# One 1024-column subtraction in place of two of 512 for the low part of a weight unit

## The reference, cut to what matters

```python
proj = h @ w_in                                     # 39 units of 128 columns in layer 0, 61 in layer 1
xbc  = silu(causal_dwconv(xbc, conv_w, conv_b))     # four taps along the tokens
...                                                 # SSD heads and window attention, or gated DeltaNet and block attention
y    = concatenate([y_a, y_b]) @ w_out              # 2048 x 1024
x    = x + g_m * rms_norm(y, norm_w)
u    = causal_dwconv(h @ w_up, conv_w, conv_b)      # three taps; w_up is 1024 x 5632
y    = (gelu(gate) * val) @ w_down                  # 2816 x 1024
```

## Time and profile before

| | |
|---|---|
| median of 3 runs | 1235.38 us (1235.38 to 1236.77) |
| the profiled execution, its own time | 1234.31 us |
| its span in the trace | 1232.5 us |
| PE busy | 1125.3 us, 91% |
| DVE busy | 883.5 us, 72% |
| ACT busy | 628.2 us, 51% |
| mean granted TensorE clock | 0.953 of 2.4 GHz |

### The profile page before, as it was taken

One profiled execution on the slowest core, in us unless ns is written; L12 is line 12 of the kernel. 1 busy time (PEld: TensorE's weight loads), 2 busy tenths in 40 slices (PEclk: granted clock), 3 DMA queues, 4 the chain that ended last, 5 costly groups with the idle time before them and its releaser, 6 DMA issues.

```text
span 1232.5 us, 28100 instructions
## 1 busy us (share of the span) xinstructions
PE 1125.3 (91%) x10161; PEld 1088.7 (88%) x10161; DVE 883.5 (72%) x1909; ACT 628.2 (51%) x1317; POOL 21.0 (2%) x12
## 2 busy tenths in 40 slices
PE   5899999989899999989999997589986989999996
PEld 5899988979899999989999985579876989999996
DVE  3587646669778889976888674876644886888854
ACT  1376455344366665445666536166524445666542
POOL 0000000000000000000000001200100000000000
PEclk9899899999889999987999998789999998999998
DMA  9457534627636566932766521013202662666661
GB/s 358 151 172 238 177 122 141 197 84 292 254 104 186 178 181 221 342 118 78 228 223 187 188 70 35 2 40 88 83 1 92 208 249 75 184 185 179 180 200 56
DMA packets 54830, 195.58 MB, mean 159 GB/s; under 512 B 6067, under 2 KB 8115, under 8 KB 54492
## 3 DMA queue, kind: packets, MB, share of 16 engines
q1 hardware_dynamic: 54748, 194.45, 48.2%
HBM read 193.36 MB, written 1.07 MB: 158 GB/s over the span
## 4 chain that ended last, share of the span: by engine, by line
PE 68%; DVE 6%; ACT 2%; issue 1%; DVEq 0%; ACTq 0%
PE proj L507 43%; PE acc L507 25%; DVE off_bd L1677 1%; DVE state L1751 1%; PE acc L688 0%; DVE sys_t L1685 0%; DVE yr L1492 0%; DVE o_tok L1778 0%; DVE yr L1469 0%; DVE k_tok L1667 0%; DVE conv L1698 0%; DVE w_lo L1345 0%; ACT w_hi L1003 0%; DVE dec L1660 0%; DVE ada_sum L1359 0%
## 5 line engine op out<-in xcount | busy, mean ns | idle before, releaser
L1003 ACT ACTIVATE w_hi<-raw 128x512 fp32r<-128x512 f32 x528 | 328.7, 625 | 178.6 <-PE acc L507 127.9
L1345 DVE TENSOR_TENSOR w_lo<-raw,w_hi 128x512 fp32r<-128x512 f32 x528 | 358.8, 684 | 79.0 <-ACT w_hi L1003 77.8
L507 PE MATMUL proj<-h_hi,w_hi 128*128 128x256 f32 x1352 | 389.8, 288 | 4.0 <-DVE h_lo L1465 3.7
L507 PE MATMUL proj<-h_lo,w_hi 128*128 128x256 f32 x1352 | 386.1, 286 | 0.0
L507 PE MATMUL proj<-h_hi,w_lo 128*128 128x256 f32 x1352 | 385.9, 285 | 0.0
L507 PEld LDWEIGHTS proj<-h_hi,w_hi 128*128 128x128 f32 x1352 | 262.9, 194 | 6.7 <-issue 4.0
L507 PEld LDWEIGHTS proj<-h_lo,w_hi 128*128 128x128 f32 x1352 | 263.5, 195 | 0.0
L507 PEld LDWEIGHTS proj<-h_hi,w_lo 128*128 128x128 f32 x1352 | 263.1, 195 | 0.0
L507 PE MATMUL acc<-a_hi,w_hi 128*128 128x256 f32 (+1 forms) x608 | 172.5, 284 | 3.6 <-DVE a_lo L1632 2.0
L507 PE MATMUL acc<-a_lo,w_hi 128*128 128x256 f32 (+1 forms) x608 | 170.4, 280 | 0.0
L507 PE MATMUL acc<-a_hi,w_lo 128*128 128x256 f32 (+1 forms) x608 | 170.3, 280 | 0.0
(11 more groups left out here) (259 smaller groups left out, 1564.3 us busy)
## 6 DMA issues: line engine op xcount, KB each, us to landing
raw<-in_w_stream SPq DMA_DIRECT2D x264, 512.0 KB, 3.6
ada_long<-in_ada_stream SPq DMA_DIRECT2D x52, 512.0 KB, 6.9
ada_first<-in_ada_stream SPq DMA_DIRECT2D x20, 512.0 KB, 4.4
ada_ssd<-in_ada_stream SPq DMA_DIRECT2D x12, 512.0 KB, 4.5
ada_out<-in_ada_stream SPq DMA_DIRECT2D x12, 512.0 KB, 4.8
hankel<-bias_scratch SPq DMA_DIRECT2D x2, 1024.0 KB, 6.1
x<-in_x_tiles SPq DMA_DIRECT2D x1, 1024.0 KB, 10.5
out_tiles<-x SPq DMA_DIRECT2D x1, 1024.0 KB, 3.9
```

Of the source, the lines that this page charges most:

```text
L507: return pe.matmul(out, a, b, start=start, stop=stop, skip_group_check=True)
L1003: act.activation(hi, src, ACT.Copy).then_inc(w_rounded, 1)
L1345: dve.tensor_tensor(lo, src, hi.bitcast(F32), ALU.subtract).then_inc(w_split, 1)
```

## The change

`split_half` does nothing any more for half 0. When it is called for half 1 it waits until both halves of the unit are rounded, forms the low part of the whole unit in one instruction of 1024 columns, and adds 2 to `w_split`. The two slots that the unit's halves take in `w_hi` and `w_lo` lie side by side, and so do the halves in `raw`, so one instruction reaches them.

```diff
             def split_half(n, a, i=0):
-                if n >= UNITS:
+
+                if n >= UNITS or a == 0:
                     return
-                hi, lo, src = w_half(n, a)
-                dve.wait_ge(w_rounded, 8 * i + 2 * n + a + 1)
-                dve.tensor_tensor(lo, src, hi.bitcast(F32), ALU.subtract).then_inc(w_split, 1)
+                s = 2 * n % 4
+                dve.wait_ge(w_rounded, 8 * i + 2 * n + 2)
+                dve.tensor_tensor(w_lo[:, s:s + 2].rearrange("p s a b -> p (s a b)"), raw[:, n % 4].rearrange("p a b -> p (a b)"),
+                                  w_hi[:, s:s + 2].rearrange("p s a b -> p (s a b)").bitcast(F32), ALU.subtract).then_inc(w_split, 2)
```

## The result

| | before | after |
|---|---|---|
| median | 1235.41 us (1235.38 to 1236.77) | 1283.68 us (1279.78 to 1289.47) |
| the profiled execution, its own time | 1234.31 us | 1282.69 us |
| its span | 1232.5 us | 1280.5 us |
| mean granted clock | 0.953 | 0.960 |

The change makes the kernel slower by a ratio of 1.0383 (95% interval 1.0356 to 1.0411). The forecast was 1284 us, with a range of 1260 to 1298.

A forecast was written before the change was run, and what follows sets the result against it. PE bounds the kernel (busy 91%, 68% of the chain); later low parts stall it in tap stages. Terms sum to 51 us on 1234.3, 1285.3; adding 1.1 to the median and taking 2 off gave 1284 us, range 1260 to 1298.

The forecast's parts named there:

- LS: Start of PE's last matmul of unit n, from which the low part's ready and due times for unit n+2 are counted.
- The bare tap wait: Conv and up stages: second tap's uncovered wait for the first, pitch 0.64 us against 0.40; ends move sum -7.7 to +7.0.
- The restart from the low part's end: A released PE starts 0.13 us after the low part's end, read at one unrolled place; in loops up to 0.12 more.
- out0: Start of out0, where PE already waits for DVE: half 0 lasts 1.22 in place of 0.70, costing 0.5 us.
- The tap stages in sum: Conv and up stages: 27.2, 7.0 and 12.2 us looped, 2 unrolled, less 2 for first units.
- The start of down1: DVE arrives late from the last up step with four terms a unit: estimated 0.9 us, likewise at down0.
- The SSD steps, the norms and what lies around them: Three norms cost 0.3 us; SSD split delays DVE at most 0.54 us, but PE takes `mmat` 0.59 later.
- The steady steps of out and down: They cost nothing: two steps stay about 6.1 us and the low part is ready 0.6 us ahead of due.
- DVE's saved time counts: Rival, in out and down: DVE holds PE back, saving at most 17 us, time 1231 us; chance 0.05.
- the cover holds: Rival, tap stages: the low part still comes in time, no change, 1234 to 1237 us; chance 0.04.
- Half the stall: Rival, tap stages: tap wait not bare and restart free, 0.18 us a unit in up, 1264 us; chance 0.11.
- The clock: Rival, tap stages: PE's pauses drop the granted clock to 1.2 GHz for parts, 1325 us; chance 0.04.

The follow-up runs named there:

- wide between the taps: Kernel after with the one 1024-column split moved back between first and second tap in conv and up stages: 1250.55 us, ratio 1.0115.
- two halves late: Kernel after with its split made as two 512-column instructions, each with its own signal, both behind the second tap: 1249.43 us, ratio 1.0101.
- one signal: DVE's instructions and order as in the kernel before, but half 0 is signalled only together with half 1: 1271.2 us, ratio 1.0267.
- later in every second: Kernel after with the split moved behind `prod` in the second unit of each pair of the up stages: 1304.78 us, ratio 1.0558.
- after, 8 more matmuls: Kernel after with eight repeated matmuls added to each unit of the conv and up stages: 1375.44 us.
- the pair with more matmuls: Eight repeated matmuls added per conv and up unit, once on the kernel before and once on the kernel after: 1367.29 and 1375.44 us.
- the fourth experiment: 1024-column split only outside conv and up, which keep two halves as in the kernel before: 1238.3 us beside 1238.26 for before, ratio 1.0008.

## Why the prediction was right

The mechanism, its place and its size were right. That the median came within 0.3 us of the forecast is luck: the tap stages lost 44.7 us for 46.4, the rest at least 5.0 for 2.6, and 1.7 of these 5.0 did not show in the span (3.3), where the granted clock was 0.960 and not 0.953. What the rest lost is in part of a kind that the sum had put at nothing.

**The round.** By it two units take the time from LS to the ready low part, plus the time from PE's restart to its next LS. With the two numbers that the trace of after corrected (PE starts 0.05 behind the low part's end, and takes 2.85 from first to last start), every variant follows in up0:

| | low part ready | round | per unit | measured per unit |
|---|---|---|---|---|
| before | LS + 2.35 | 5.20, under 5.76 | 2.88 | 2.878 |
| wide between the taps | LS + 2.95 | 5.80 | 2.90 | 2.930 |
| two halves late | LS + 2.97 | 5.82 | 2.91 | 2.937 |
| one signal | LS + 3.34 | 6.19 | 3.10 | 3.114 |
| after | LS + 3.51 | 6.36 | 3.18 | 3.196 |
| later in every second | LS + 3.98 | 6.83 | 3.42 | 3.420 |
| after, 8 more matmuls | LS + 3.51 | 7.32 (3.51 + 2.85 + 0.96), under 7.68 | 3.84 | 3.838 |

The measured column is the mean over ACT's taps from the fifth to the last. The two variants at LS + 2.95 and 2.97 lose 0.05 to 0.06 us a unit where the due time alone, LS + 3.00, would give nothing: a low part must be there somewhat before the matmul that needs it. The weight load that goes ahead of the matmul is what waits in their traces, by some 0.1 us once in two units. I have no run that tells the size of this lead apart from the restart.

**Point by point.**

- The bare tap wait, taken at 0.64 between 0.52 and 0.75: a pair of taps lasts 1.11, so its pitch is 1.11 - 0.48 = 0.63 in up. In the conv stages it is more, 79.81 - 79.14 = 0.67 (below). The split took 1218 ns for a forecast of 1.22 us.
- The restart from the low part's end, taken from out0 as 0.13, was 0.05 in the loops. This is the term of the sum that was mis-sized most: 0.08 a round, 0.04 a unit, 5 us over 128 units. The second matmul came 0.22 behind the first, not 0.20.
- up: 0.34 a unit forecast, 3.196 - 2.878 = 0.318 measured. conv0: 0.44 and 3.301 - 2.858 = 0.443; the round there gives 3.30 a unit by the corrected terms, and 0.02 of the 0.443 come from before, which took 2.858 and not 2.88. conv1: 0.38 and 3.236 - 2.880 = 0.356.
- The tap stages in sum: 46.4 for the looped units, 2 for the unrolled, less 2 for the first units, is 46.4 against 44.7.
- out0: 0.5 forecast. PE waited 2.26 us where it had waited 1.67, 0.59 more (PE's timeline of the kernel after stands below). The start of down1: 0.9 forecast and some 0.1 for its norm; 78.86 - 77.58 = 1.28 measured. down0 has the same two waits of 0.45 and 0.15 us, yet its stretch came out 0.55 us shorter than before, at a mean clock of 0.93 against 0.90. Its cost can be read at its start, where the clock was 1.00 in both. From up0's last tap to the first matmul behind the second wait it was 480.47 - 472.33 = 8.14 us before and 501.78 - 492.37 = 9.41 after, 1.27 more. In the pair with more matmuls, at 0.93 in both, the whole stretch is 99.68 against 97.82 us.
- The SSD steps, the norms and what lies around them: 0.3 us were forecast for three norms and nothing for the rest. The kernel after has the same delays as the fourth experiment, 0.61 at `ada_sum`, 0.61 at `mmat`, 0.51 at the norm behind conv1 and 0.47 in the attention: 2.2 us. The forecast had read `mmat` as ready 0.59 us ahead of PE in one SSD step. In the step at 202 us it had no such lead, and the split's longer time went to PE whole. One step was not enough to set this term to nothing.
- The steady steps of out and down: two steps of DVE take 6.1 us, from the split at 302.57 to the second next at 308.66 below, as forecast, and PE does not wait there. PE's own pace is 2.82 us a unit there, 5.63 for two, so that DVE falls behind by 0.46 in two steps, before as after; the stage ends before that costs a wait for the split.
- Waits in one unit of two, which was one of the two forms named. Their total, forecast as some 45 us, is 40.4 by the weight loads' row and 27.2 by PE's.

PE's timeline of the kernel after at the start of out0:

```profile
288.43 0.36 PE L507 MATMUL acc<-a_hi,w_hi 128*128 128x256 f32 x1 [2.26 <-DVE w_lo L1346]
```

DVE's timeline of the kernel after, in conv0 and in out0:

```profile
79.14 0.48 DVE L1400 SCALAR_TENSOR_TENSOR conv<-proj,prm,conv 128x255 f32 x1 [1.36 <-ACT conv L1035]
79.81 0.48 DVE L1400 SCALAR_TENSOR_TENSOR conv<-proj,prm,conv 128x254 f32 x1 [0.18 <-DVE conv L1400]
80.21 1.22 DVE L1346 TENSOR_TENSOR w_lo<-raw,w_hi 128x1024 fp32r<-128x1024 f32 x1
...
302.57 1.22 DVE L1346 TENSOR_TENSOR w_lo<-raw,w_hi 128x1024 fp32r<-128x1024 f32 x1
...
308.66 1.22 DVE L1346 TENSOR_TENSOR w_lo<-raw,w_hi 128x1024 fp32r<-128x1024 f32 x1
```

**The rivals.** That DVE's saved time counts fell: DVE is 3.8 us less busy and the kernel 48 slower, and where the wide form stands alone it gains nothing and makes PE stand 5.0 us longer. One reason that the forecast gave against it was misread: by its own rows the operation does get cheaper per column when wider, 1.34 ns at 512 columns, 1.24 at 768 and 1.14 at 1536. What rules out 1024 columns in 0.6 us is that every wider one took longer as a whole, and it took 1.22. That the cover holds fell with the 60 waits. Half the stall assumed a covered tap wait, and it is not covered. The clock was 1.00 in all four tap stages.

The Trainium skill, "Perfetto Trace Analysis", section "Optimizing Scalar/DVE Operations", says that breaking up instructions may let work be completed sooner where the engine is not saturated but holds others up. The trace agrees: the two halves behind the second tap lose 10.8 us in the tap stages, one instruction in the same place 44.7. With eight more matmuls a unit the same merge cost 0.3 us there, so what it costs hangs on the due time as well.

The Trainium skill, "TensorE: Matmul & The Clock Gate", section "A second HAM failure mode: psum-queue depth-cycling", reports a kernel whose short idles made the clock swing. Here PE paused for some 0.6 us in every 6.4 and was granted 1.00 throughout up1, so the trace does not bear it out for this kernel.

## What to carry to other kernels

Ahead of merging two instructions, look at when the first one's signal is due: the merged one signals at its end, from the place of the second, and what it saves in pitch (0.065 us here) is small beside what the signal loses (1.2 us). Write down the cover from the waiter's due time and the time line of one round; if two slots are under way, a delay beyond the cover costs half per unit, and the slower of the two slots paces both. Where there is cover, the merge costs nothing, but it also brings nothing unless that engine bounds. Ask for the cover of all that stands behind the merged instruction in its engine's queue: outside the tap stages four of seven delays hit a matmul that waited for other work of DVE, not for the split. And compare the granted clocks ahead of calling two medians the same.

## What the runs showed that I had not expected

- PE starts 0.05 us behind the end of the low part inside the loops (422.05 for a split that ends at 420.78 + 1.22), but 0.13 at the unrolled out0 and 0.15 at the unrolled down1 of the fourth experiment. A single place is not enough for a term that is multiplied by 64.
- A chained tap has a pitch of 0.63 us in up and 0.67 in conv, with register work between, against 0.52 for a chained term.
- Kernels with the same code in a stretch get another clock there: 0.89, 0.93 and 1.00 in the 46 us behind conv0, and 3 us of time between the last two. One kernel differs too: 20 executions of before had a mean clock of 0.946 to 0.958 and took 1241.4 to 1229.6 us. The tap stages repeat within 0.05 us in kernels with the same code there; the rest of the span moves by several us. A difference of spans of less than that is better read stage by stage, or matmul by matmul at places where both clocks are 1.00.
